# Moving the A and GLU tiles of the first head pair, and the whole first convolution, to before and beside the second column half of V

## The reference, cut to what matters

```python
h = _rmsnorm(x, norm_g)                       # 512 + 1024 tokens, 1024 channels
proj = h @ w_in                               # 9 blocks of 1024 columns
a_val, a_glu, z_a, q, k, v, z_b, g_logits = split(proj)
u = a_val * sigmoid(a_glu)
c = depthwise_conv(u, dw_w, width=31) + dw_b
y_a = (silu(layernorm(c)) * silu(z_a)) @ w_pw_a
attn = neighbourhood_attention(q, k, v, rpb)  # 16 heads of 64, window 8 x 16 on a grid 64 wide, bias rpb
y_b = (attn * silu(z_b)) @ w_o_b
y = x + (sigmoid(g_a) * y_a + sigmoid(g_b) * y_b) @ w_out    # then a final RMSNorm
```

## Time and profile before

| | |
|---|---|
| median of three runs | 1823.62 us (1823.16 to 1826.27) |
| the profiled execution | 1826.82 us |
| its span, first to last instruction | 1825.0 us |
| PE busy | 1795.5 us, 98% of the span |
| DVE busy | 1092.7 us, 60% |
| ACT busy | 549.9 us, 30% |
| mean granted TensorE clock | 0.994 |

### The profile page before, as it was taken

One profiled execution on the slowest core, in us unless ns is written; L12 is line 12 of the kernel. 1 busy time (PEld: TensorE's weight loads), 2 busy tenths in 40 slices (PEclk: granted clock), 3 DMA queues, 4 the chain that ended last, 5 costly groups with the idle time before them and its releaser, 6 DMA issues.

```text
span 1825.0 us, 25369 instructions
## 1 busy us (share of the span) xinstructions
PE 1795.5 (98%) x9164; PEld 1462.4 (80%) x9164; DVE 1092.7 (60%) x1573; ACT 549.9 (30%) x1117; POOL 210.5 (12%) x250
## 2 busy tenths in 40 slices
PE   7999999999999999999999999999999999999998
PEld 6888778888888888888888888888887777888886
DVE  4400794875677378468558738756874666535432
ACT  4411134233233223323322332341344233203122
POOL 1210011011011001101101110110110055000001
PEclk9999999999999999999999999999999999999999
DMA  7263012312312311221221123123126656533223
GB/s 279 68 117 89 24 36 65 87 53 82 88 36 81 93 36 64 81 77 58 86 77 42 64 71 82 52 81 87 35 72 246 236 165 195 172 132 104 93 81 127
DMA packets 163357, 174.03 MB, mean 95 GB/s; under 512 B 11238, under 2 KB 117750, under 8 KB 163098
## 3 DMA queue, kind: packets, MB, share of 16 engines
q1 hardware_dynamic: 137034, 112.11, 20.7%
q10 hardware_dynamic: 22320, 46.41, 6.8%
q0 software_dynamic: 3872, 13.75, 3.0%
HBM read 121.55 MB, written 50.68 MB: 94 GB/s over the span
## 4 chain that ended last, share of the span: by engine, by line
PE 90%; DVE 5%; DMA 3%; issue 1%; ACT 1%; SPq 0%; POOL 0%; POOLq 0%; ACTq 0%; DVEq 0%
PE pg L1364 65%; PE pg L1382 14%; PE pO L1478 3%; PE pT L1463 3%; PE pS L1453 3%; DVE work L1258 1%; DMA qk<-gb_d 1%; DVE work L1072 1%; DMA work<-tb_d 1%; DVE ws L987 1%; DVE xs L995 0%; ACT xs L763 0%; DVE work L1264 0%; DMA raw<-in_w_in 0%; ACT ws L635 0%
## 5 line engine op out<-in xcount | busy, mean ns | idle before, releaser
L1364 PE MATMUL pg<-xs,ws 128*128 128x512 f32 x5760 | 1383.9, 396 | 6.8 <-DVE work L1275 6.8
L1364 PEld LDWEIGHTS pg<-xs,ws 128*128 128x128 f32 x5760 | 1067.1, 189 | 234.5 <-issue 14.8
L1072 DVE SCALAR_TENSOR_TENSOR work<-work 128x1551 f32<-128x1551 f32 x240 | 449.4, 1872 | 4.1
L1382 PE MATMUL pg<-ws,xs 128*128 128x512 f32 x1008 | 238.8, 393 | 3.2 <-DVE ws L987 1.9
L1382 PEld LDWEIGHTS pg<-ws,xs 128*128 128x128 f32 x1008 | 189.4, 189 | 44.4 <-DVE ws L987 4.4
L987 DVE TENSOR_TENSOR ws<-raw,ws 128x1024 fp32r<-128x1024 f32 x90 | 109.8, 1221 | 133.9 <-ACT ws L635 133.7
L1146 DVE CUSTOM_DVE_ANT_0 work<-pS,work 128x384 f32<-128x384 f32 (+1 forms) x192 | 88.7, 510 | 165.7 <-PE pS L1453 165.3
L584 POOL TENSOR_TENSOR work<-work 128x384 f32<-128x384 bf16 (+1 forms) x72 | 63.1, 876 | 1050.7 <-DVE small L1146 1039.7
L841 ACT ACTIVATE work<-work,small 128x384 f32<-128x384 f32 (+1 forms) x192 | 109.2, 570 | 217.7 <-DVE small L1146 217.7
L849 ACT ACTIVATE work<-pT 128x384 f32<-128x384 f32 (+1 forms) x192 | 87.2, 454 | 170.4 <-PE pT L1463 170.4
L635 ACT ACTIVATE ws<-raw 128x1024 fp32r<-128x1024 f32 x90 | 94.6, 1053 | 104.4 <-PE pg L1364 83.3
(11 more groups left out here) (100 smaller groups left out, 961.4 us busy)
## 6 DMA issues: line engine op xcount, KB each, us to landing
raw<-in_w_in SPq DMA_DIRECT2D x70, 512.0 KB, 3.8
work<-v_d SPq DMA_DIRECT2D x128, 96.0 KB, 2.9
v_d<-work ACTq DMA_DIRECT2D x24, 256.0 KB, 2.0
za_d<-work ACTq DMA_DIRECT2D x24, 256.0 KB, 2.0
ga_d<-work ACTq DMA_DIRECT2D x24, 256.0 KB, 2.0
gb_d<-work ACTq DMA_DIRECT2D x24, 256.0 KB, 2.0
work<-c_d POOLq DMA_DIRECT2D x8, 768.0 KB, 13.1
qk<-gb_d SPq DMA_DIRECT2D x24, 256.0 KB, 4.1
```

The costliest lines, as they stand in the source:

```text
L1072: nc.vector.scalar_tensor_tensor(cv[:, 0:CLEN], u[:, k:k + CLEN], cur[:, k:k + 1], cv[:, 0:CLEN], ALU.mult, ALU.add).then_inc(tap_ok, 1)
L1364: last = nc.tensor.matmul(pg[b][:], wt(s, wpart)[:, k * P:(k + 1) * P], xs[:, k, xpart, chunk(n)], start=(k == 0 and wpart == 1), stop=(k ...
L1382: last = nc.tensor.matmul(pg[b][:], xs[:, k, xpart, t * P:(t + 1) * P], wt(s0 + k // 2, wpart)[:, chunk(k % 2)], start=(k == 0 and xpart = ...
```

## The change

PE's order becomes V columns 0 to 511, A, GLU, V columns 512 to 1023, Q, K, `unit(0)`. Pieces are renumbered: 4 is A (in the spare slot, part of `qk`), 5 is GLU, 6 to 9 are the second half of V, 10 is Q, 11 is K; 12 and 13 stay ZB and ZA. All 31 taps and the copy into `csum` are done in one run on DVE while PE makes the second half of V; `unit(0)` has none. ACT's and DVE's lists follow. On SP, A and GLU are loaded where pieces 4 and 5 were, pieces 6 and 7 stand where they stood, pieces 8 and 9 are now rows of V and stand behind the wait on `rel_out` and behind `load_rel`, as the pieces of these numbers did; the table of the second head is loaded after V's last use of slot 3, `load_v` after it, and only then pieces 12 and 13.

```diff
-G_PRO = 2 * NT
-G_UNIT = G_PRO + 4 * NCH
+G_A = NT
+G_GLU = G_A + NCH
+G_V2 = G_GLU + NCH
+G_Q = G_V2 + NT
+G_K = G_Q + NCH
+G_UNIT = G_K + NCH
...
+S_A, S_GLU, S_V2 = 4, 5, 6
+S_Q, S_K = S_V2 + 4, S_V2 + 5
+S_UNIT = S_K + 1
...
-    if s < S_PRO + 1:
-        return (0, 1, 2, 3, X_SLOT, 0, 1, 2, 3)[s]
+    if s < S_Q:
+        return (0, 1, 2, 3, X_SLOT, 0, 1, 2, 3, X_SLOT)[s]
...
     if isinstance(i, int) and i == 0:
-        n, slot = TAPS - EARLY0, min(slot, 12)
-        return range(EARLY0 + n * slot // 12, min(EARLY0 + n * (slot + 1) // 12, TAPS))
+        return ()
...
-            for s in range(4, 6):
-                piece_s(s, w_rows(w0, C_V * P + CH, s - 4))
+            for s, c in ((S_A, C_A), (S_GLU, C_GLU)):
+                piece_s(s, w_tile(w0, c * P))
...
-            for s in range(6, 8):
-                piece_s(s, w_rows(w0, C_V * P + CH, s - 4))
+            for s in range(S_V2, S_V2 + 2):
+                piece_s(s, w_rows(w0, C_V * P + CH, s - S_V2))
...
             sp.wait_ge(x_lo, 3 * KT)
             sp.wait_ge(rel_out, 16 * QB)
             load_rel(0, 0, (0,))
-            for s, c in ((8, C_A), (9, C_GLU), (10, C_Q), (11, C_K)):
+            for s in range(S_V2 + 2, S_Q):
+                piece_s(s, w_rows(w0, C_V * P + CH, s - S_V2))
+            for s, c in ((S_Q, C_Q), (S_K, C_K)):
                 piece_s(s, w_tile(w0, c * P))
 
+            sp.wait_ge(w_used, 6)
+            load_rel(0, 0, (1,))
             for n in range(3):
                 sp.wait_ge(st_out[n], 128)
             load_v(0, 0)
-
-            sp.wait_ge(g_done, piece_done(S_PRO))
-            load_rel(0, 0, (1,))
-            for s, c in ((12, C_ZB), (13, C_ZA)):
+            for s, c in ((S_UNIT, C_ZB), (S_UNIT + 1, C_ZA)):
                 piece_s(s, w_tile(w0, c * P))
...
                 elif s == 9:
-                    free_sem, free = w_used, 6
-                elif s == 10:
-                    free_sem, free = w_used, 5
-                elif S_PRO + 2 < s < S_YB:
+                    free_sem, free = g_done, G_A + NCH
+                elif s == S_Q:
+                    free_sem, free = g_done, G_GLU + NCH
+                elif s == S_K:
+                    free_sem, free = w_used, 4
+                elif S_K < s < S_YB:
                     free_sem, free = g_done, piece_done(s - 2)
...
+                if NT <= g < NT + NCH:
+
+                    act.wait_ge(u_ok, g - NT + 1)
                 nc.scalar.activation(stage[:, g % 3, :], pg[b][:], ACT.Copy, scale=0.5).then_inc(g_out[b], 1)
...
-            for s in range(5, 8):
-                split_s(s)
-            take_v(NT - 1)
-            for t in range(NT):
-                take_v(NT + t)
-                if t == 4:
-                    split_s(8)
-            split_s(9)
...
+            split_s(S_GLU)
+            take_v(NT - 1)
+            for s in range(S_V2, S_V2 + 3):
+                split_s(s)
             act.wait_ge(pads_ok, 3)
-
-            act.wait_ge(rel_out, 16 * QB)
             for n in range(NCH):
-                take_a(*grs(G_PRO + n)[:2], n)
-            split_s(10)
+                take_a(*grs(G_A + n)[:2], n)
+            split_s(S_V2 + 3)
             for n in range(NCH):
-                b, done, _ = grs(G_PRO + NCH + n)
+                b, done, _ = grs(G_GLU + n)
                 act.wait_ge(g_done, done)
-                act.wait_ge(st_out[n], 128)
+                act.wait_ge(st_out[n], 64)
                 nc.scalar.activation(stage[:, n, :], pg[b][:], ACT.Tanh, scale=0.5).then_inc(g_out[b], 1)
-            split_s(11)
+            split_s(S_Q)
+            for t in range(NT):
+                take_v(NT + t)
+            split_s(S_K)
             for n in range(NCH):
-                take_q(*grs(G_PRO + 2 * NCH + n)[:2], n)
-            split_s(12)
+                take_q(*grs(G_Q + n)[:2], n)
+            split_s(S_UNIT)
             for n in range(NCH):
-                take_k(*grs(G_PRO + 3 * NCH + n)[:2], n)
+                take_k(*grs(G_K + n)[:2], n)
...
             load_taps(0, 0)
-            split_s(10)
+            split_s(S_V2 + 3)
             for n in range(NCH):
-                glu(grs(G_PRO + n), grs(G_PRO + NCH + n), n)
-            split_s(11)
+                glu(grs(G_A + n), grs(G_GLU + n), n)
+            split_s(S_Q)
+            for k in range(TAPS):
+                tap(0, k)
+            add_conv(0)
+            split_s(S_K)
             for n in range(NCH):
-                tap(0, 2 * n)
-                tap(0, 2 * n + 1)
-                take_q_lo(grs(G_PRO + 2 * NCH + n)[0], n + 1, n)
-            split_s(12)
+                take_q_lo(grs(G_Q + n)[0], n + 1, n)
+            split_s(S_UNIT)
             for n in range(NCH):
-                for k in range(3):
-                    tap(0, 2 * NCH + 3 * n + k)
-                take_k_lo(grs(G_PRO + 3 * NCH + n)[0], NCH + n + 1, n)
-            for k in range(5 * NCH, EARLY0):
-                tap(0, k)
+                take_k_lo(grs(G_K + n)[0], NCH + n + 1, n)
```

More of the change, by code:

```diff
@@ L75 @@
 G_OUT = G_YA + 24
-S_PRO = 8
-S_UNIT = S_PRO + 4
+S_A, S_GLU, S_V2 = 4, 5, 6
+S_Q, S_K = S_V2 + 4, S_V2 + 5
+S_UNIT = S_K + 1
 S_UNIT1 = S_UNIT + 6
@@ L93 @@
 EARLY = 11
-EARLY0 = 17
 def wslot(s):
-    if s < S_PRO + 1:
-        return (0, 1, 2, 3, X_SLOT, 0, 1, 2, 3)[s]
+    if s < S_Q:
+        return (0, 1, 2, 3, X_SLOT, 0, 1, 2, 3, X_SLOT)[s]
     if s >= S_OUT + 4:
@@ L143, in piece_done @@
 def piece_done(s):
-    return G_PRO + 3 * (s - S_PRO) + 3
+    return G_Q + 3 * (s - S_Q) + 3
 def build(nc, x_prompt, x_sample, norm_g, w_in, b_gate, dw_w, dw_b, ln_g, ln_b, w_pw_a, rpb,
@@ L673, in take_v @@
             def take_v(g):
-                b, done, out = grs(g)
+                b, done, out = grs(g if g < NT else G_V2 + g - NT)
                 act.wait_ge(g_done, done)
@@ L803, in evac @@
                         act.wait_ge(u_ok, 3 * i + (n + 1))
+                        if first:
+                            act.wait_ge(st_out[n], 128)
                         nc.scalar.activation(st, pg[b][:], ACT.Tanh, scale=0.5).then_inc(th_ok, 1)
@@ L1045, in _ @@
             nc.vector.memset(u[:, ULEN - PAD:ULEN], 0.0).then_inc(pads_ok, 1)
-            for s in range(5, 8):
+            for s in range(S_GLU, S_V2 + 2):
                 split_s(s)
@@ L1049, in _ @@
             nc.vector.tensor_copy(par[:].rearrange("p k n -> p (k n)"), pS[0][:, 0:KT * NPAR]).then_inc(par_ok, 1)
-            for s in range(8, 10):
-                split_s(s)
+            split_s(S_V2 + 2)
             def load_taps(ct, before):
@@ L1213, in unit @@
                             tap(i, k)
-                    if slot == BLK:
+                    if slot == BLK and not (isinstance(i, int) and i == 0):
                         add_conv(i)
@@ L1414, in _, with tile_group @@
             params()
+            def tile_group(g, s, n):
+                if n == 0:
+                    pe.wait_ge(w_lo, s + 1)
+                pe.wait_ge(g_out[g % 2], g // 2)
+                half_group(g % 2, s, n, 0)
+                half_group(g % 2, s, n, 1).then_inc(g_done, 1)
+            for g0, s in ((G_A, S_A), (G_GLU, S_GLU)):
+                for n in range(NCH):
+                    tile_group(g0 + n, s, n)
             for t in range(NT):
-                token_group(NT + t, 4, t, 0, False)
-            for m in range(4):
+                token_group(G_V2 + t, S_V2, t, 0, False)
+            for g0, s in ((G_Q, S_Q), (G_K, S_K)):
                 for n in range(NCH):
[L1419 to L1424, removed]
+                    tile_group(g0 + n, s, n)
             def column_sums(part, taken):
```

## The result

The changed kernel took 1844.32 us (median of six runs, 1840.65 to 1846.38), the kernel before beside it 1825.76 us (six runs, 1823.16 to 1826.91): a ratio of 1.0101, 95% interval 1.0086 to 1.0116, so 15.7 to 21.2 us slower. The forecast was 1841.1 us, range 1835 to 1846. The profiled execution of the changed kernel has a span of 1841.5 us, 16.5 us over that of before.

A forecast was written before the change was run, and what follows sets the result against it. PE, busy 98% of the span, was taken to bound the kernel. Stall 20.7 plus clock 2.0 less 5.2 won gives + 17.5 us on the median 1823.6: 1841.1 us, range 1835 to 1846.

The forecast's parts named there:

- The stall: PE before the third A group, waiting for take_a behind ACT's split of piece 8: 20.7 us, bounds 19.3 to 22.2.
- both conditions that the prediction named: Piece 8 lands late behind SP's table wait, and ACT's list has its split ahead of take_a(0).
- T: Time at which piece 8 lands: forecast 119.3 us, against 120.83 before; PE resumes at T + 1.6.
- the stores' 2.9 us: Most that T could fall if the table's writes gained the moved V stores' DMA share; half, 1.5 us, was taken.
- the stall of 19.3 us: PE's stall before the third A group if, by the skill's queue rule, the table gained close to the stores' share.
- Clock: PE's loss at the low clock after the stall: 2.0 us, bounds 1.5 and 3.4.
- Waits won: PE's two waits around unit(0), 2.20 + 1.28 us, and 1.7 us of low clock vanish: 5.2 us, at least 3.9.
- The parts costed at nothing: Taps run beside V's second half, about 20 us spare; second head's table and ZB's piece beside Q and K, 12 spare.
- the table speeds up by more: Rival: table's write is mostly contention; T 105.0 to 110.9, stall 6.4 to 12.3 us, 1827 to 1833 us; chance 0.08.
- the one of waits that stay: Rival: unit(0)'s waits stay, held by another DVE duty or ZB's late piece; adds up to 5.2 us, 1846; chance 0.04.
- no second stall: After the third A group PE stands no more: split 9 follows take_a(2) on ACT and GLU(0) is 5.4 us long.
- The case on the other side: Rival: not slower, piece 8 lands before PE needs bank 0, only the gain stands, 1818.4 us; chance 0.03.

The follow-up runs named there:

- e2: Changed kernel, SP's list untouched, splits of pieces 8 and 9 moved behind GLU's evacuations on ACT and DVE: 1820.3 us, ratio 0.9969 to the kernel before.
- e8: Changed kernel with pieces 8 and 9 issued ahead of SP's table wait, and POOL writing the table only once piece 8 is split: 1820.43 us, ratio 0.9968.
- e4: Changed kernel with the eight loads of the table's first head moved behind pieces 8 and 9 on SP: 1840.08 us, one run.
- e3: Changed kernel with splits of pieces 8 and 9 between A's and GLU's evacuations on ACT: 1827.66 us, ratio 1.0012 to the kernel before.
- e6: Changed kernel with four 256 KB stores to an unused buffer, issued by SP behind piece 7 in place of the moved V stores: 1846.67 us, one run.
- e1: Changed kernel with pieces 8 and 9 issued by SP right behind 6 and 7, ahead of the table wait: 1827.25 us, ratio 1.0013 to the kernel before.
- e7: Kernel before, with k's last low part made ahead of the last three taps on DVE: 1827.07 us, ratio 1.0011.
- e5: Changed kernel with the sixteen writes of the bias table issued by SP in place of POOL: 1839.69 us, one run.

## Why the prediction was right

**The place.** The stall came where it was put: third A group, from 100.8 us, released by `take_a`, behind the split of piece 8, behind SP's wait of 24.0 us for the table. e2 takes the stall away by the order on ACT and DVE alone (SP's list untouched), e8 by an early landing alone (ACT's order untouched): both conditions that the prediction named are needed. e4 shows that the time of landing sets the stall's length, e3 that it counts only from where PE runs out of banks.

**The terms.** Stall 20.7 forecast, 20.09 measured; T 119.3 forecast, 119.34 measured. That T was met so closely is luck: half of the stores' 2.9 us was a choice between ends, and with the same transfers the table's time varies by 1.7 us between executions (under e6). The executions with the stores are all slower (25.0 us and more against 24.8 and less), so the direction is supported; the size of 1.4 us is no larger than that spread. The rule of the Trainium skill (DMA: Bandwidth & Descriptors, "Queues, rings and completion order") goes with e6 and e1 in direction: who adds packets delays the other, piece 8 by 7.4 us in e1. No run shows the turns themselves, and the stall of 19.3 us that the prediction drew from it was 20.09. Clock 2.0 forecast, 1.7 measured; that was the low end, since e1 and e3 paid 3.0 at the same kind of stop. Waits won 5.2 forecast; in the profiled spans 20.1 + 1.7 - 5.2 = + 16.6, measured + 16.5. That a sum meets the difference of two single executions so closely is luck too: the medians lie 18.6 us apart. e2 gives the gain alone: 5.4 us by the medians (interval 3.5 to 7.9), forecast 5.2.

**What was off.** The forecast of 1841.1 stood on a median of before of 1823.6; with more runs it is 1825.8, and 2.1 of the 3.2 us between forecast and result are that. The remaining 1.1 us (+ 17.5 forecast, + 18.6 measured) is within the interval.

**The parts costed at nothing** were so: the taps and their copy ended at 205.4 us, V at 210.3; ZB's piece was issued at about 222, and unit(0) has no wait. The rival "the table speeds up by more" fell (1.4 us), the one of waits that stay fell (none at unit(0)), and no second stall followed. The case on the other side would have needed the piece at 102 us; even e1, which issues it 23 us earlier, did not quite bring it by then.

**A prediction of mine that failed** is that of e1, where the table's writes were taken as no obstacle to a load: the 3.9 us of piece 7 were measured just as the writes began, and were carried over to a time when they were in full course. Two smaller ones: e7's wait grew more than forecast, and the table written by SP (e5) fell between the two theories.

## What to carry to other kernels

When work is moved ahead in time, look at each in-order list for what was harmless there because its successor was far off: a split of a weight piece that waits for a DMA may stand ahead of a PSUM evacuation only if the DMA lands before PE comes back to that bank. In e8 it landed at 96 us, needed by about 99, and cost nothing; in the changed kernel it landed at 119 and cost 20 us. Trace the DMA back through its issuing queue too, since a wait for something unrelated (here the bias table) passes on through two lists. And a load moved to an earlier place takes the landing time of its new neighbours: an earlier load took 16 of the stall's 20 us away, and what was left ate the whole gain, until the writes beside it were moved as well.

## What the runs showed of the hardware

**The price of the low clock did not grow with the length of the stop.** The 24 matmuls after the stop took, against 5.44 us: 7.17 after 20.1 us of idle time, 7.33 after 16.4 (e5), 8.07 after 16.1 (e4), 7.99 after 23.3 (e6), 8.45 after 4.4 (e1), 8.49 after 5.75 (e3). That is 1.7 to 3.1 us, in no order of the idle time. When the clock fell does not settle the price either. After the stop of 20.1 us it had fallen long before PE started again (0.50 over 115 to 120 us), and it was high again by 125. In e1 it fell only at the end of the stop (0.89 over 100 to 105), and PE ran the whole of 105 to 110 at 0.50. But in e6 it was at 0.50 from 110 us on, also long before, and the price was 2.6 us. Why it came back sooner in one than in another no row shows. The forecast's bounds of 1.5 to 3.4 hold all six. That the default is the slow state, as TensorE: Matmul & The Clock Gate of the Trainium skill says ("What's actually happening"), goes with a price that does not grow.

**Executions of one kernel spread by 5 us and more, and part of it arises far from the change.** The six of e2 lie between 1818.8 and 1825.1 us. e8 and e2, equal by their medians within 0.2 us, have spans of 1818.6 and 1823.2 us. The window of 25 us from 1450 on, first e8, then e2 (length, PE, PEld, DVE, ACT, POOL, clock, DMA share, GB/s):

```profile
1450.00:1475.00 25.00, 22.34 (x98) 17.31 (x97) 14.36 (x13) 8.37 (x11) 3.98 (x4) 0.93 0.38 118
```

```profile
1450.00:1475.00 25.00, 22.34 (x88) 17.98 (x86) 13.73 (x12) 6.03 (x6) 2.30 (x1) 0.80 0.30 87
```

At the same busy time e2 made 88 matmuls in place of 98, at a granted clock of 0.80 in place of 0.93 (0.13 of 25 us: 3.2 us). What made the clock differ there is open. A change worth 0.3% is told by medians and by the waits at its own place, not by two spans.
